# Stick-breaking attention in a two-layer trunk: logits of two query rows in one piece of TensorE work, sigmoid and scans in SBUF

## What is computed

```
z = einsum('bhqd,bhkd->bhqk', qb, kb) * scale
mask = kpos < qpos                                        # strictly causal
log_keep = where(mask, log_sigmoid(-z), 0)
suffix = cumsum(log_keep, axis=3, reverse=True) - log_keep   # sum over s < j < t
weights = where(mask, exp(log_sigmoid(z) + suffix), 0)
out = einsum('bhqk,bhkd->bhqd', weights, vb)
```

## Time and profile before

| | |
|---|---|
| median of 3 runs | 2921.53 us (2921.23 to 2926.58) |
| profiled execution, its own time | 2921.85 us |
| its span, first to last instruction of the slowest core | 2920.1 us (8 cores: 2896.3 to 2920.1) |
| TensorE busy | 2797.7 us, 96% |
| VectorE, ScalarE, GpSimd busy | 1436.4, 1261.6, 1602.0 us (49, 43, 55%) |
| chain that ended last | TensorE 79%, DMA 6%, VectorE 6%, issue 4%, GpSimd 3%, ScalarE 2% |

### The profile page before, as it was taken

The page is one execution under the profiler, slowest core; times in us unless marked ns, Lnnn a source line. Parts: engine busy times, 40 slices in busy tenths (PEclk is TensorE's granted clock), DMA queues, the critical chain, the costliest instruction groups (busy, mean ns, idle before and its releaser), DMA issues.

```text
span 2920.1 us, 43942 instructions; the slowest of 8 cores (2896.3 to 2920.1 us)
## 1 busy us (share of the span) xinstructions
PE 2797.7 (96%) x13211; PEld 1194.9 (41%) x13211; DVE 1436.4 (49%) x1759; ACT 1261.6 (43%) x2062; POOL 1602.0 (55%) x1793
## 2 busy tenths in 40 slices
PE   8999999999999999799998999999999989999998
PEld 3444444444443344343443444444444434444443
DVE  4411246464435555776645454445565675554003
ACT  3433234736335344365543353433645464444231
POOL 4655515765417777576761465550576766674333
PEclk9999999999999999899999999999999999999999
DMA  8798883456665999746755344465355485446222
GB/s 171 157 208 196 177 216 90 120 150 147 184 155 107 193 177 175 190 123 157 167 139 155 85 107 113 114 157 170 92 123 123 106 216 135 114 114 184 86 77 83
DMA packets 491478, 420.24 MB, mean 144 GB/s; under 512 B 310128, under 2 KB 334960, under 8 KB 491248
## 3 DMA queue, kind: packets, MB, share of 16 engines
q1 hardware_dynamic: 465184, 370.07, 49.1%
q0 software_dynamic: 26064, 47.36, 11.3%
HBM read 304.23 MB, written 89.13 MB: 135 GB/s over the span
## 4 chain that ended last, share of the span: by engine, by line
PE 79%; DMA 6%; DVE 6%; issue 4%; POOL 3%; ACT 2%; SPq 1%; DVEq 0%; POOLq 0%; ACTq 0%
PE ps L588 74%; PE ps L1349 3%; PE ps L1402 2%; DMA stg<-xT 2%; DMA ring<-wblk 1%; DVE vt L1209 1%; DVE P L1365 1%; DMA h<-xT 1%; POOL Wq L1379 1%; DMA Wk<-Wq 1%; SPq L581 1%; DVE X L746 1%; POOL ps L1064 1%; DMA ring<-wbf 1%; POOL ffB L937 0%
## 5 line engine op out<-in xcount | busy, mean ns | idle before, releaser
L588 PE MATMUL ps<-X,ring 128*128 128x512 bf16 x6144 | 1399.1, 383 | 36.3 <-DVE X L746 11.1
L588 PEld LDWEIGHTS ps<-X,ring 128*128 128x128 bf16 x6144 | 586.0, 98 | 778.9 <-issue 121.5
L1379 POOL TENSOR_TENSOR Wq<-P 128x1024 bf16<-128x1024 f32 (+2 forms) x320 | 529.1, 1655 | 299.3 <-DVE P L1365 289.7
L588 PE MATMUL ps<-mix,ring 128*128 128x512 bf16 x2816 | 657.0, 380 | 7.2 <-POOL P L1360 4.1
L1365 DVE TENSOR_TENSOR_SCAN P<-ps,carry,cbs 128x512 f32<-128x512 f32 x384 | 488.9, 1279 | 346.1 <-POOL P L1360 200.6
L578 ACT ACTIVATE ps<-ps 128x512 f32<-128x512 f32 (+3 forms) x576 | 429.6, 750 | 477.4 <-PE ps L588 238.2
L588 PE MATMUL ps<-ffB,ring 128*128 128x512 bf16 x2048 | 485.1, 380 | 0.0
L811 DVE TENSOR_TENSOR tmp<-ps,ms 128x512 f32<-128x512 f32 x256 | 175.3, 685 | 494.0 <-PE ps L588 493.3
L816 POOL TENSOR_TENSOR h<-tmp,h 128x512 f32<-128x512 f32 x224 | 287.7, 1284 | 229.9 <-DVE tmp L811 229.1
L588 PEld LDWEIGHTS ps<-mix,ring 128*128 128x128 bf16 x2816 | 263.8, 98 | 339.7 <-issue 39.6
L1365 DVE TENSOR_TENSOR_SCAN P<-ps,cbs 128x128 f32<-128x128 f32 (+3 forms) x256 | 208.1, 819 | 323.6 <-ACT ps L578 189.4
(11 more groups left out here) (82 smaller groups left out, 1755.2 us busy)
## 6 DMA issues: line engine op xcount, KB each, us to landing
ring<-wbf SPq DMA_DIRECT2D x540, 256.0 KB, 3.0
ring<-wblk POOLq DMA_DIRECT2D x180, 256.0 KB, 7.9
wbf<-ring SPq DMA_DIRECT2D x180, 256.0 KB, 6.4
stg<-xT SPq DMA_DIRECT2D x96, 256.0 KB, 4.8
h<-xT SPq DMA_DIRECT2D x64, 256.0 KB, 7.4
hsp<-h SPq DMA_DIRECT2D x64, 256.0 KB, 3.7
h<-hsp SPq DMA_DIRECT2D x64, 256.0 KB, 6.2
oT<-mixf SPq DMA_DIRECT2D x32, 256.0 KB, 5.1
```

The source lines that it names most:

```text
L588: ins = pe.matmul(out, lhsT=l, rhs=r, start=(first and i == 0), stop=(last and i == n - 1), skip_group_check=True)
L1379: yield Req("pool", lambda e: e.tensor_tensor(out=W4, in0=P[:, :, 1:w + 1].rearrange("p h (j n) -> p h j n", n=128), in1=P[:, :, 0:w].rear ...
```

## The change

The logits of rows r and r + 1 of a group become one request of four matmuls, which needs both PSUM pairs at once. The sigmoid reads PSUM and writes the product tile P in SBUF, after which the PSUM pair is free (before: after the scans). The scans then read and write P in place. Some of the planner's cost numbers are changed; they move no work by themselves, but the order of all queues follows from them.

```
-DMA_KB_US = 256.0
+DMA_KB_US = 230.0
...
 def att_item(self, s, u, x):
-        il = tq * 4 + r
-        zs = yield self.zsets
+        k0 = c * 512
+        if r % 2 == 0:
+            z0 = yield self.zsets
+            z1 = yield (self.zsets,)
+            G["z"] = {r: z0, r + 1: z1}
+            n0, n1 = (((r + 1) * 128, (r + 2) * 128) if first else (512, 512))
+
+            def zmm(pe):
+                ins = None
+                for zs, rr, wr in ((z0, r, n0), (z1, r + 1, n1)):
+                    for h in range(2):
+                        hp = slice(h * 64, (h + 1) * 64)
+                        il = tq * 4 + rr
+                        ins = pe.matmul(self.ps[zs][:, h * 512:h * 512 + wr], lhsT=self.qT[hp, a, il * 128:(il + 1) * 128],
+                                        rhs=self.kT[hp, a, k0:k0 + wr], start=True, stop=True, skip_group_check=True)
+                return ins
+            yield Req("pe", zmm, [self.LqT[a][tq], self.LkT[a][c]], [self.Lbank[2 * z + i] for z in (z0, z1) for i in range(2)],
+                      (n0 + n1) / 2400.0 + 0.33, bias=-0.04, wslack=0.5)
+            G["zr"] = r + 1
+        yield lambda: G.get("zr", 0) >= r
+        zs = G["z"][r]
         p = yield self.p_P
...
-        yield self.act(z3, z3, AF.Sigmoid, [], Lz, 2 * w, True, scale=-0.125)
+        yield self.act(self.P[:, p, :, 0:w], z3, AF.Sigmoid, [], Lz + [self.LP[p]], 2 * w, True, scale=-0.125)
+        self.zsets.free(zs)
...
             yield Req("dve", (lambda h: lambda e: e.tensor_tensor_scan(
-                out=P[:, h, 0:w][:, ::-1], data0=zt[:, h * 512:h * 512 + w][:, ::-1], data1=low[:, ::-1],
+                out=P[:, h, 0:w][:, ::-1], data0=P[:, h, 0:w][:, ::-1], data1=low[:, ::-1],
                 initial=1.0 if first else self.carry[:, pv["cy"], h:h + 1], op0=ALU.mult, op1=ALU.max))(h),
-                [self.Lz0, self.Lcb] + ([] if first else [self.Lcarry[pv["cy"]]]), [LP, Lz[h]], w * 2.15e-3 + 0.19)
-        self.zsets.free(zs)
+                [self.Lz0, self.Lcb] + ([] if first else [self.Lcarry[pv["cy"]]]), [LP], w * 2.15e-3 + 0.19)
...
-                  [LWq], [LWk[r]], 1.25, key=("wk", k, r), lat=4.0, kb=w * 0.69)
+                  [LWq], [LWk[r]], 1.22, key=("wk", k, r), lat=1.6, kb=w * 0.4)
...
-                      0.15 + 0.216 * (2.5 if first else 4), bias=-0.04, slack=4.0)
+                      0.45 + 0.216 * (2.5 if first else 4), bias=-0.04, slack=4.0)
```

More of the change, by code:

```diff
@@ L634, in keep_block @@
     def keep_block(self, slot, b):
-        yield self.dma(self.wbf[b], self.ring[:, slot, :], [self.Lring[slot]], [self.Lwbf[b]], ("keep", slot), kb=150.0)
+        yield self.dma(self.wbf[b], self.ring[:, slot, :], [self.Lring[slot]], [self.Lwbf[b]], ("keep", slot), kb=170.0)
         self.busy.discard(slot)
@@ L689, in square @@
             yield Req("pool", lambda e: e.tensor_tensor(out=Xf[:, SQ[i][odd], hs], in0=sq, in1=sq, op=ALU.mult), Ls,
-                          [LX[k][t] for k in rows[odd]], 1.15, bias=0.5)
+                          [LX[k][t] for k in rows[odd]], 1.06, bias=0.5)
         else:
@@ L703, in square @@
                 in0=Xf[:, SQ[i][0], hs], in1=Xf[:, SQ[i][1], hs], op=ALU.add),
-                [LX[k][t] for k in rows[1]], [LX[k][t] for k in rows[0]], 0.70 if eng == "dve" else 1.15)
+                [LX[k][t] for k in rows[1]], [LX[k][t] for k in rows[0]], 0.72 if eng == "dve" else 1.29)
             ev.sums.add(i)
@@ L814, in evac @@
             self.banks.free(bk)
-            eng, d = ("dve", 0.70) if last and c >= 6 else ("pool", 1.15)
+            eng, d = ("dve", 0.71) if last and c >= 6 else ("pool", 1.29)
             yield Req(eng, lambda e: e.tensor_tensor(out=self.h[:, c, ts], in0=self.tmp[:, b, :], in1=self.h[:, c, ts],
@@ L937, in evac @@
                     yield Req("pool", lambda e: e.tensor_tensor(out=F[:, jj, ts], in0=m, in1=m, op=ALU.mult),
-                              [self.Ltmp[b]], [LF[jj][t]], 1.15)
+                              [self.Ltmp[b]], [LF[jj][t]], 1.06)
                     self.p_tmp.free(b)
@@ L1065, in evac @@
                     out=S1[:, b0:528][:, ::-1], in0=src[:, b0:528][:, ::-1], in1=src[:, b0 - d:528 - d][:, ::-1],
-                    op=ALU.add))(src, d, b0), [Ls], [L1], 1.15)
+                    op=ALU.add))(src, d, b0), [Ls], [L1], 1.2)
                 src, Ls = S1, L1
```

## The result

The changed kernel takes 3081.98 us in the median (3080.95 to 3083.75), 1.0547 times the kernel before (95% interval 1.0529 to 1.0565): about 160 us slower. The prediction had the sign and the mechanism, and a size of 66 us. Runs in which one die was slowed are left out of all ratios.

What follows compares the result with a forecast made beforehand. TensorE, busy 96% of the span, was taken to set the time. 2921.85 us, plus 79 for turns, less 13 kept of 27 for breaks, with moved waits and cost numbers at nothing, gave 2988, said as 2990; range 2890 to 3075.

Steps and rivals of the forecast that it cites:

- The breaks: TensorE's main stream: pairing logits saves 134 breaks at 0.2 us, 27 us gained, 13 us of it counted.
- The turns: Scans with two SBUF inputs alternate with POOL's operations: stretches three, five and six grow by 32, 28, 19, +79 us.
- one to six: Stretches of the span with scans: 442-760, 868-1178, 1210-1520, 1640-1960, 2050-2325 and 2365-2620 us.
- Then stretch two fits (306 of 310): Stretch two, 868 to 1178 us: at 0.92 full, turns need 306 of its 310 us, so no growth.
- the need of the prediction: Per stretch: POOL's busy time (DMA issues left out in two) plus scans, less 0.13 us per operation counted.
- The 0.92: How full turns of DVE and POOL can run in a stretch, taken about midway between 0.86 and full.
- The moved waits: POOL's copies and memsets wait for ACT's sigmoids: nothing to 1.01 us for each of 160 pairs, taken as nothing.
- The cost numbers: Changed planner numbers reorder queues everywhere, adding no instruction: put at 0, within 6 us either way.
- That scans don't take turns: Rival: scans on DVE lose nothing beside POOL and the breaks count in full, 2895 us; chance 0.17.
- That turns pack almost fully: Rival: turns fill DVE's and POOL's idle time; at 0.99 growth and gain cancel, at 1.00 2915 us; chance 0.08.
- That POOL's queue is held for sigmoids: Rival: no turns, but copies waiting for sigmoids hold POOL's queue for 80 us, 2915 to 2975 us; chance 0.06.
- the upper bound: Top of the range, 3075 us: turns only 0.86 full, stretches two, three, five, six grow 161 us, net about +153.

Runs made afterwards that it cites:

- the two kernels without turns: Sigmoid to SBUF, scans' constant in PSUM, two main banks: one row at a time 1.0369, rows paired with new cost numbers 1.0285, against the kernel before.
- the control pair: Changed kernel with two main PSUM banks instead of three, scans' constant in SBUF: 1.0903; same order of instructions, constant read from PSUM: 1.0285.

## Why the prediction was right in kind and wrong in size

**The breaks (27 us).** About right: 25 us in the two kernels without turns, in which the new cost numbers are counted; alone these lose 9. The prediction let 13 of the 27 count where turns are the bound. Sigmoid and scans in SBUF alone have 1.0597, all parts together 1.0547, so 15 us were kept, cost numbers counted again; the two ratios' intervals overlap, so this is no more than roughly right.

**The turns (+79 us).** The mechanism is shown by the place of one constant. The term was mis-sized: sigmoid and scans in SBUF alone cost 0.0597, 174 us, and the pair with two banks gives 181. Laid out by stretch, with the 13 us shared out by scans, the forecast was -4, -5, +32, -4, +28 and +19 us for one to six, and +9, +32, +42, +4, +36 and +26 were measured, and +11 between five and six. Of the 94 us missed, 37 lie in stretch two, 25 in three, five and six, 21 in one and four and 11 in the seam.

Three steps made the term small. The first is "Then stretch two fits (306 of 310)". With the need of the prediction, turns came out at 282 us in 345, 0.82 full, in stretch two, 315 in 353 (0.89) in three, 279 in 311 (0.90) in five and 252 in 281 (0.90) in six. The 0.92 was a little high for three, five and six, and taken for the whole of stretch two it let idle time at one end pay for a crowd at the other. In the kernel before, the third of five equal parts of stretch two reads, for all engines, for scans and for POOL's DMA issues:

```profile
992.00:1054.00 62.00, 62.00 (x306) 25.83 (x305) 35.81 (x39) 16.07 (x27) 53.08 (x59) 1.00 1.14 188
...
992.00:1054.00 62.00, 27.23 (x25) 1.00 1.14 188
...
992.00:1054.00 62.00, 8.90 (x16) 1.00 1.14 188
```

Its need is 53.1 - 8.9 + 27.2 less 68 x 0.13, 62.6 us of 62: full, in a stretch that is 0.91 on the average. The queues have a fixed order, so work can't move to the emptier end. With 0.92 and all five parts looked at by themselves, only 12 of the 32 us of stretch two come out, 6 each in parts three and four. In the changed kernel these two parts, found by their main matmuls, are where 9 and 14 us are lost. Some 8 us of stretch two are the lower clock, by the estimate above; the rest was not traced to a cause.

The second step is that nothing was put for the stretches below 0.92 and the seams: +9 and +4 instead of -4 each in one and four, +11 between five and six. (For stretch one the need also left out its 16 instructions of line 847, two of which are those of the earlier trace rows: with them it is 265 of 318, 0.83, still far from full.)

The third is that the forecast left TensorE's clock where it was, at 0.98 to 1.00: it went to 0.95 to 0.99, an estimated 37 us in all, spread over the stretches. That turns bring this about is shown by the control pair: with one order of instructions the clock over the cores is 0.967 to 0.971 with turns and 0.981 to 0.985 without.

**The moved waits (nothing).** Too small by about 9 us, hardly more than the intervals tell: waits for copies cost 18 us in the changed kernel and 9 in the kernel before, although POOL was waiting for turns. The early freeing of PSUM pairs, priced at little, seems to be what lets the pairing gain anything: 25 us with it, none without. Those kernels differ in main banks and cost numbers too, so this isn't shown by itself.

**The cost numbers (0, within 6 us).** 9 us slower in the kernel before, interval 4 to 15.

**The sum.** Sigmoid and scans in SBUF 174 us, which holds the waits of the copies and the lower clock, pairing with cost numbers -25: 149, against 160 measured. The parts were measured in different surroundings, with intervals of some 11 us each way, and add up within these.

**The rivals.** That scans don't take turns is refuted by the control pair. That turns pack almost fully is refuted by 0.82 to 0.90. That POOL's queue is held for sigmoids is a part of it, some 9 us more than before, and can't stand alone. The time, 3082, lies 7 us over the upper bound, which was set at 0.86 for stretches two, three, five and six. That it lies so near is luck: the bound had 161 us for these four, where 136 were measured, and -8 us for one, four and the seam, where 24 were. TensorE's busy time grew by 20 us although it has 27 us of breaks less, of which the lower clock accounts for some 10 (37 less 27). Idle time alone doesn't set that clock: the kernel before has 0.983 to 0.987 over its cores with TensorE idle for 122 us, the kernel with the constant in PSUM and two main banks 0.981 to 0.985 with 207, the changed kernel 0.971 to 0.975 with 264. Which of the waits bring it down is open.

## What to carry to other kernels

Before moving an operand of a DVE operation from PSUM to SBUF, count its tensor inputs in SBUF and look at what POOL does meanwhile: with two of them scans and POOL's operations took turns here, and it was enough to put a constant into PSUM to end that. Judge a shared resource by short pieces and not by the average of a stage, since queues of fixed order can't shift work, and expect a loss before it is full: stretch one grew by 9 us at a need of 0.83. If the waits reach TensorE, what its clock then loses comes on top. A gain on the bounding engine is only kept if the buffers that it asks for come free in time.

## Not expected of the hardware

A scan whose data lie in SBUF and whose constant is read from PSUM, one column over and over, takes 1275 to 1278 ns on the mean, as one with its data in PSUM and its constant in SBUF (1279). One main PSUM bank less costs this kernel 3.7%. POOL's DMA issues (line 622) kept their median of 567 ns and their maximum of 742 beside scans with two SBUF inputs, so that they don't show turns.
